# RWKV core: the triangular inverse through four quarters of the array, its X update in bank 6

## What is computed

```python
def step(state, inp):
    r_t, w_t, k_t, v_t, kk_t, b_t = inp
    sk = jnp.einsum('bhvk,bhk->bhv', state, kk_t)
    state = (state * w_t[:, :, None, :] - sk[..., None] * b_t[:, :, None, :]
             + v_t[..., None] * k_t[:, :, None, :])
    return state, jnp.einsum('bhvk,bhk->bhv', state, r_t)
...
_, o = lax.scan(step, s0, (seq_first(r_h), seq_first(w_h), seq_first(k_h), seq_first(v_h),
                           seq_first(kk), seq_first(kk * a_h)))
```

## Time and profile before

| | us |
|---|---|
| median of 3 runs | 3152.23 (3150.76 to 3156.98) |
| span of the profiled execution | 3153.8 |
| PE busy in it | 2975.0 (94%) |
| DVE, POOL, ACT busy | 1542.3, 865.3, 588.5 |
| the RWKV core's blocks, first LT product to the last copy of O | 1038 to 1343 |

### The profile page before, as it was taken

One profiled execution on the slowest core, in us unless ns is written; L12 is line 12 of the kernel. 1 busy time (PEld: TensorE's weight loads), 2 busy tenths in 40 slices (PEclk: granted clock), 3 DMA queues, 4 the chain that ended last, 5 costly groups with the idle time before them and its releaser, 6 DMA issues. The chain is left out here.

```text
span 3153.8 us, 52317 instructions
## 1 busy us (share of the span) xinstructions
PE 2975.0 (94%) x22150; PEld 2086.0 (66%) x22150; DVE 1542.3 (49%) x2520; ACT 588.5 (19%) x1102; POOL 865.3 (27%) x591
## 2 busy tenths in 40 slices
PE   9999999999999899999999998999879998999998
PEld 6845857986887688658566685677768844443433
DVE  5764756336555467534777664764644332111112
ACT  2142040012001333210100002221443211110101
POOL 1111222111121545211899790011245310000000
PEclk9999999999999899999999999999999998999999
DMA  4342223220321000042334452132200017999996
GB/s 165 94 165 77 80 82 113 81 80 28 127 87 47 3 3 4 36 135 74 126 127 148 155 164 80 56 102 68 74 9 3 22 60 271 381 409 409 409 409 272
DMA packets 122230, 412.64 MB, mean 131 GB/s; under 512 B 13568, under 2 KB 21376, under 8 KB 121744
## 3 DMA queue, kind: packets, MB, share of 16 engines
q1 hardware_dynamic: 112784, 373.64, 33.3%
q0 software_dynamic: 9216, 35.66, 3.4%
HBM read 404.97 MB, written 4.28 MB: 130 GB/s over the span
## 5 line engine op out<-in xcount | busy, mean ns | idle before, releaser
L947 PE MATMUL ps<-arena 128*128 128x256 f32 x4760 | 1044.3, 381 | 18.0 <-PEq L905 6.8
L947 PEld LDWEIGHTS ps<-arena 128*128 128x128 f32 x4760 | 898.8, 191 | 173.9 <-issue 43.9
L1003 PE MATMUL ps<-arena 128*128 128x512 f32 (+1 forms) x752 | 291.5, 546 | 10.4 <-DVE arena L1342 7.3
L885 POOL TENSOR_TENSOR arena<-arena 128x512 f32<-128x512 f32 x68 | 94.1, 1384 | 555.9 <-DVE arena L903 190.5
L1003 PEld LDWEIGHTS ps<-arena 128*128 128x128 f32 x752 | 144.3, 193 | 149.6 <-issue 138.7
L3895 PE MATMUL ps<-arena 128*64 128x512 f32 x1024 | 224.8, 594 | 9.7 <-DMA arena<-in_w_up 7.2
L891 POOL TENSOR_TENSOR arena<-arena 128x512 f32<-128x512 f32 x68 | 86.5, 1271 | 484.7 <-PE ps L947 484.7
L1247 DVE TENSOR_TENSOR arena<-ps,arena 128x256 f32<-128x256 f32 x85 | 36.1, 425 | 331.1 <-PE ps L947 330.1
L1178 DVE SCALAR_TENSOR_TENSOR arena<-ps,params,arena 128x511 f32<-128x511 f32 (+4 forms) x266 | 190.7, 717 | 13.5 <-ACT arena L1079 4.4
L4039 POOL TENSOR_SCALAR arena<-arena,small 128x1024 f32<-128x1024 f32 x64 | 191.5, 2992 | 10.1 <-DMA arena<-in_w_mod 6.4
L3895 PEld LDWEIGHTS ps<-arena 128*64 128x64 f32 x1024 | 83.7, 137 | 149.2 <-issue 148.8
(11 more groups left out here) (453 smaller groups left out, 4047.6 us busy)
## 6 DMA issues: line engine op xcount, KB each, us to landing
arena<-in_w_in SPq DMA_DIRECT2D x166, 512.0 KB, 3.7
arena<-in_w_gate SPq DMA_DIRECT2D x128, 512.0 KB, 15.5
arena<-in_w_up SPq DMA_DIRECT2D x128, 512.0 KB, 15.3
arena<-in_w_down SPq DMA_DIRECT2D x128, 512.0 KB, 15.4
arena<-in_w_mod POOLq DMA_DIRECT2D x48, 512.0 KB, 4.2
arena<-in_ffn_up SPq DMA_DIRECT2D x44, 512.0 KB, 4.0
arena<-in_w_branch SPq DMA_DIRECT2D x32, 512.0 KB, 3.6
arena<-spill POOLq DMA_DIRECT2D x16, 640.0 KB, 5.3
```

Source lines behind the costliest of these rows:

```text
L885: vec.tensor_tensor(plane(u, n), part(u, 1, 0), part(u, 1, 1), ALU.add).then_inc(sem, 1)
L947: last = nc.tensor.matmul(k.bank(b)[:, 0:HT], lhs[:, q * P:(q + 1) * P], rhs[:, q, :], start=(first and q == 0), stop=(q == 3), skip_group ...
L1003: last = nc.tensor.matmul(out[0:j["m"], 0:j["n"]], w[:, q * m:(q + 1) * m], j["rhs"](q), start=(n == 0), stop=(n == kn - 1))
```

## The change

- X and XT are kept mirrored to each other. XT keeps the layout of before (partition half = half q of the chunk, columns by head), X and Y take the other (partition half = head h, columns by q). So Y = LM times XT and XT's update X times Y go from each half to both, over four quarters into banks 0 and 1 (level 5: banks 2 and 3). The new helpers are `to_heads` and `to_chunks`. X0 (a product with the identity) and Y5, XT5 go the same way.
- X's own update (X1 to X4) is `in_heads`: two quarters, into bank 6. Bank 6 is also that of the spread norms, the turned O and the bonus, so waits are added in both directions.
- The order on a level is Y, XT, X instead of Y, X, XT.
- `step_lt` makes L twice, as it is and transposed, the second into columns 256 to 511 of the same banks. On DVE it is three operations as before; the mirrored L (`LS`) is what POOL masks for the levels.
- B's order is Y5, trv, XT5, Lk, trkap, trkt, LkV, trbt, NU0, WT, Ak, Ab, with Y5 and XT5 on both banks.
- The turn of O moves from beat 10 to 9, weighed from 12 to 10, the bonus from 14 to 13, its addition from 15 to 14. In the last block they stay at 7, 12, 11 and 15.

```diff
@@ -2025,7 +2025,7 @@
...
-    LT, LM, X, XT, Y = (lambda p, n=n: own(5 * (p % 2) + n) for n in range(5))
+    LS, LM, X, XT, Y = (lambda p, n=n: own(5 * (p % 2) + n) for n in range(5))
@@ -2041,11 +2041,15 @@
...
-    two_banks = lambda b: k.ps[:, b:b + 2, 0:256].rearrange("p h (i c) -> p h i c", i=TT)
+    two_banks = lambda b, o=0: k.ps[:, b:b + 2, o:o + 256].rearrange("p h (i c) -> p h i c", i=TT)
+    pair = lambda ap: ap.rearrange("p (n c) -> p n c", n=2)
+    both = lambda b: k.ps[:, b:b + 2, 0:256]
+    turned_cell = lambda q, i: slice(256 * q + 64 * i, 256 * q + 64 * i + 64)
...
-    strict, incl, ident = k.const("strictC"), k.const("inclC"), k.const("identC")
-    level = lambda n: k.const("levelC")[:, 64 * n:64 * n + 64]
+    strict, incl, ident, after = k.const("strictC"), k.const("inclC"), k.const("identC"), k.const("strictTC")
+    level = lambda n: k.const("levelTC")[:, 64 * n:64 * n + 64]
+    first_level = k.const("levelC")[:, 0:64]
@@ -2061,11 +2065,13 @@
...
-    A = ["X0"] + [f"{s}{n}" for n in (1, 2, 3, 4) for s in ("Y", "X", "XT")]
-    B = ["trv", "Y5", "trkap", "XT5", "Lk", "trkt", "LkV", "trbt", "NU0", "WT", "Ak", "Ab"]
-    B_BEAT = [0, 0, 2, 2, 3, 4, 5, 6, 6, 7, 9, 11]
-    B_BANKS = [(3,), (2,), (3,), (2,), (2, 3), (3,), (2,), (3,), (2,), (2, 3), (2, 3), (2, 3)]
+    A = ["X0"] + [f"{s}{n}" for n in (1, 2, 3, 4) for s in ("Y", "XT", "X")]
+    B = ["Y5", "trv", "XT5", "Lk", "trkap", "trkt", "LkV", "trbt", "NU0", "WT", "Ak", "Ab"]
+    B_BEAT = [0, 1, 2, 3, 4, 5, 5, 6, 6, 7, 9, 11]
+    B_BANKS = [(2, 3), (2,), (2, 3), (2, 3), (2,), (3,), (2,), (3,), (2,), (2, 3), (2, 3), (2, 3)]
+    X_BANK = 6
...
+    TURN_BEAT, WEIGHED_BEAT, BONUS_BEAT, ADDED_BEAT = (9, 7), (10, 12), (13, 11), (14, 15)
@@ -2132,11 +2138,11 @@
...
-            def products(l, r, b):
+            def products(l, r, b, at=0):
...
-                        ins = nc.tensor.matmul(k.bank(b + h)[half(q), 64 * i:64 * i + 64], l[half(h), t], r[half(h), t], start=True, stop=True)
+                        ins = nc.tensor.matmul(k.bank(b + h)[half(q), at + 64 * i:at + 64 * i + 64], l[half(h), t], r[half(h), t], start=True, stop=True)
@@ -2146,12 +2152,26 @@
...
-            def blocks64(l, r, b):
-                for h in range(2):
+            def to_heads(l, r, b):
+                for i in range(TT):
+                    for q, h in ((0, 0), (1, 1), (0, 1), (1, 0)):
+                        other = k.const("ident")[half(q), half(q)] if r is None else r[half(q), cell(h, i)]
+                        ins = nc.tensor.matmul(k.bank(b + q)[half(h), 64 * i:64 * i + 64], l[half(q), cell(h, i)], other, start=True, stop=True)
+                return ins
+
+            def to_chunks(l, r, b):
+                for i in range(TT):
+                    for h, q in ((0, 0), (1, 1), (0, 1), (1, 0)):
+                        t = turned_cell(q, i)
+                        ins = nc.tensor.matmul(k.bank(b + h)[half(q), 64 * i:64 * i + 64], l[half(h), t], r[half(h), t], start=True, stop=True)
+                return ins
+
+            def in_heads(l, r, b):
+                for q in range(2):
...
-                        for q in range(2):
-                            other = k.const("ident")[half(q), half(q)] if r is None else r[half(q), cell(h, i)]
-                            ins = nc.tensor.matmul(k.bank(b)[half(q), cell(h, i)], l[half(q), cell(h, i)], other, start=True, stop=True)
+                        for h in range(2):
+                            t = turned_cell(q, i)
+                            ins = nc.tensor.matmul(k.bank(b)[half(h), t], l[half(h), t], r[half(h), t], start=True, stop=True)
@@ -2164,25 +2184,34 @@
...
-                b = A.index(s) % 2
+                n = int(s[-1])
...
-                    ins = blocks64(XT(p), None, b)
+                    ins = to_heads(XT(p), None, 0)
...
-                    n = int(s[1:])
...
-                    pe.wait_ge(*a_out(p, f"X{n - 1}"))
-                    ins = blocks64(LM(p), X(p), b)
+                    pe.wait_ge(*a_out(p, f"XT{n - 1}" if n > 1 else "X0"))
+                    ins = to_heads(LM(p), XT(p), 0)
...
-                    pe.wait_ge(*a_out(p, "Y" + s[2:]))
-                    ins = blocks64(Y(p), XT(p), b)
+                    pe.wait_ge(*a_out(p, f"Y{n}"))
+                    if n > 1:
+                        pe.wait_ge(*a_out(p, f"X{n - 1}"))
+                    ins = to_chunks(X(p), Y(p), 0)
...
-                    pe.wait_ge(*a_out(p, "Y" + s[1:]))
-                    if s != "X1":
-                        pe.wait_ge(*a_out(p, f"XT{int(s[1]) - 1}"))
-                    ins = blocks64(XT(p), Y(p), b)
+                    pe.wait_ge(*a_out(p, f"Y{n}"))
+                    if n == 1:
+                        pe.wait_ge(kap_ok, min(p + 2, PAIRS))
+                        if p >= 1:
+                            pe.wait_ge(*a_out(p - 1, "X4"))
+                    else:
+                        pe.wait_ge(*a_out(p, f"X{n - 1}"))
+                    if p >= 3 and n == 3:
+                        pe.wait_ge(weighed, p - 2)
+                    if p >= 3 and n == 4:
+                        pe.wait_ge(bonus_ok, p - 2)
+                    ins = in_heads(Y(p), X(p), X_BANK)
@@ -2196,11 +2225,12 @@
...
-                    pe.wait_ge(*a_out(p, "X4"))
-                    ins = cells(LM(p), X(p), b)
+                    pe.wait_ge(*a_out(p, "XT4"))
+                    ins = to_heads(LM(p), XT(p), b)
...
-                    ins = cells(Y(p), XT(p), b)
+                    pe.wait_ge(*a_out(p, "X4"))
+                    ins = to_chunks(X(p), Y(p), b)
@@ -2266,7 +2296,8 @@
...
-                products(pl(a + p), pl(sg + p), 2).then_inc(lt_made, 1)
+                products(pl(a + p), pl(sg + p), 2)
+                products(pl(sg + p), pl(a + p), 2, 256).then_inc(lt_made, 1)
@@ -2340,16 +2371,21 @@
...
+                        if b >= 2:
+                            pe.wait_ge(*a_out(b - 2, "X4"))
...
-                    if b >= 4 and beat == (10 if b < BLOCKS - 1 else 7):
+                    if b >= 4 and beat == TURN_BEAT[b == BLOCKS - 1]:
...
+                        pe.wait_ge(*a_out(min(b - 1, PAIRS - 1), "X2" if b < PAIRS + 1 else "X4"))
...
-                    if b >= 4 and beat == (14 if b < BLOCKS - 1 else 11):
+                    if b >= 4 and beat == BONUS_BEAT[b == BLOCKS - 1]:
...
+                        if b < PAIRS + 1:
+                            pe.wait_ge(*a_out(b - 1, "X3"))
@@ -2384,7 +2420,7 @@
...
-                nc.scalar.activation(Y(p) if s[0] == "Y" else X(p), k.bank(A.index(s) % 2), ACT.Copy).then_inc(a_act, 1)
+                nc.scalar.activation(pair(Y(p) if s[0] == "Y" else X(p)), both(0), ACT.Copy).then_inc(a_act, 1)
@@ -2393,8 +2429,10 @@
...
+                elif s == "Y5":
+                    ins = nc.scalar.activation(pair(Y(p)), both(2), ACT.Copy)
...
-                    dst = {"Y5": Y(p), "trv": VT(p), "trkap": KAPT, "trkt": KT_(p), "trbt": BT_(p), "LkV": LKV}[s]
+                    dst = {"trv": VT(p), "trkap": KAPT, "trkt": KT_(p), "trbt": BT_(p), "LkV": LKV}[s]
@@ -2467,7 +2505,7 @@
...
-                tt(eight(LM(p)), eight(LT(p)), mask8(level(n)), ALU.mult).then_inc(lm_ok if n <= 4 else lm5_ok, 1)
+                tt(eight(LM(p)), eight(LS(p)), mask8(level(n)), ALU.mult).then_inc(lm_ok if n <= 4 else lm5_ok, 1)
@@ -2530,7 +2568,10 @@
...
-                nc.vector.tensor_tensor(x, x, k.bank(A.index(s) % 2), ALU.subtract).then_inc(a_dve, 1)
+                if s[1] == "T":
+                    nc.vector.tensor_tensor(pair(x), pair(x), both(0), ALU.subtract).then_inc(a_dve, 1)
+                else:
+                    nc.vector.tensor_tensor(x, x, k.bank(X_BANK), ALU.subtract).then_inc(a_dve, 1)
@@ -2538,7 +2579,7 @@
...
-                    ins = nc.vector.tensor_tensor(XT(p), XT(p), k.bank(2), ALU.subtract)
+                    ins = nc.vector.tensor_tensor(pair(XT(p)), pair(XT(p)), both(2), ALU.subtract)
@@ -2551,10 +2592,10 @@
...
-                nc.vector.tensor_tensor(quad(LT(p)), two_banks(2), mask(strict), ALU.mult).then_inc(lt_read, 1)
+                nc.vector.tensor_tensor(quad(XT(p)), two_banks(2), mask(first_level), ALU.mult)
+                nc.vector.tensor_tensor(quad(LS(p)), two_banks(2, 256), mask(after), ALU.mult).then_inc(lt_read, 1)
...
-                link(nc.vector.scalar_tensor_tensor(out=eight(XT(p)), in0=eight(LT(p)), scalar=-1.0, in1=mask8(level(0)), op0=ALU.mult, op1=ALU.mult))
-                nc.vector.tensor_tensor(eight(XT(p)), eight(XT(p)), mask8(ident), ALU.add).then_inc(lt_out, 1)
+                nc.vector.tensor_tensor(eight(XT(p)), mask8(ident), eight(XT(p)), ALU.subtract).then_inc(lt_out, 1)
@@ -2611,11 +2652,11 @@
...
-                elif beat == 12:
+                elif beat == WEIGHED_BEAT[p == PAIRS - 1]:
...
-                elif beat == 15:
+                elif beat == ADDED_BEAT[p == PAIRS - 1]:
```

## The result

The changed kernel takes 3173.2 us (median of 4 runs, 3167.5 to 3180.5) against 3154.3 for the kernel before, measured beside it (3150.8 to 3157.0): ratio 1.0056, 95% interval 1.0042 to 1.0071. It is slower by 18 us, where 7 were forecast. 3173.2 lies in the range of 3138 to 3177 and above the forecast's own range (3154 to 3166).

The account below looks back on a forecast made before the run. PE was taken to set the pace in beats 5 to 14, chains through ACT and DVE in beats 15 to 4. Block terms of +4.25 us plus clock losses of 1.7 and 1.4 gave +7.3, so 3159.5 us; range 3138 to 3177.

Parts of the forecast that it names:

- The walk through a full block: One full block, from one state product of beat 15 to the next: 36.07 us against 33.65, 2.4 us longer.
- The two new waits: PE waits for DVE's reads of X2 and X3 in bank 6: 0.85 us before the turn, 0.9 before the bonus.
- Blocks 4 to 7: The four full blocks with all parts: 4 x 2.4 = +9.7 us for the order, with clock losses added separately.
- the sum outside them: Other blocks' order terms: block 3 -2.5, block 2 -0.65, block 8 -0.8, block 9 0, block 0 +1.0, block 1 -2.5 us.
- block 2: Walked like the full block and block 3: -0.65 us, with no clock loss charged to it.
- rival A: PE's saving across eight pairs is paid out in full, 36 us: 3116 us. Chance 0.10.
- Block 8: The block without LT and exponentials: 29.0 us against 29.80, so -0.8.
- Block 1: A bare chain of Y, ACT, XT and DVE with X beside it, 22.03 us before: -2.5 us, between 0 and -5.
- block 3: Has chunk steps but no turn and no bonus, 33.40 us before: -2.5 us, plus 0.35 for the clock.
- D: New-form products stay at 0.93 us, so the 0.45 saving is missing: +20 us, or 3180. Chance 0.05.
- B: Waits on bank 6 are covered, four blocks lose 2.6 instead of 9.7: 3152 us, or 3143 if the clock holds. Chance 0.27.
- C: The clock falls around beat 0: 2.0 us more for each of blocks 4 to 7, block 1 gains nothing: 3170. Chance 0.18.

Follow-up runs that it names:

- e4_fill: The changed kernel with 32 unread identity products into bank 6 ahead of trkap in blocks 2 to 7: 3165.9 us, ratio 1.0038 to the kernel before.
- e1_beats: The changed kernel with the turn of O back at beat 10 and the bonus at 14, weighed 11, addition 15: 3156.8 us, ratio 1.0006 to the kernel before.
- e7_turn_only: The changed kernel with only the turn of O back at beat 10, weighed at 11, bonus still at 13: 3162.4 us, ratio 1.0026 to the kernel before.
- e9_dense: The kernel before with 12 four-quarter, then 12 two-quarter steps added back to back ahead of LT in block 2, unread: 3181.1 us in a single run.

## Why the prediction was right in direction and short in size

*The walk through a full block* held. The pieces of blocks 5 and 6, each read where the clock was whole or within 0.02 of it, add up to 36.5 us against 36.07 forecast. (Block 4 ran at 1.00 and took 35.33, as trkap stands 11.41 behind the copy there.) Counted from the O copy: trv 2.99 (forecast 2.79), XT5's read 8.07 (7.97), trkap 12.48 (12.38), from there to WT 7.33 (7.22), WT to the next copy 16.68 (16.47). The two new waits are 0.88 and 0.77 us (0.85 and about 0.9). LT's read to the state product took 2.4 us (2.52). DVE was the engine that I had working through from XT5 to Lk, and it was.

*Blocks 4 to 7* were to lose 9.7 for the order and 2.8 for the clock: 12.5. They lost 12.6 in one profile and 14.1 in the other. An estimate of the split: the order takes 36.5 - 33.65 = 2.85 in each of blocks 5 to 7 and 1.9 in block 4 (35.33 against 34.64 less the 1.2 of its dip before), so 10.5, and the clock the other 2.2 and 3.6. That 4 x 2.4 came so near is in part luck: block 4 lost less than the walk said, the others more. A dip costs 1.4 to 2.75 us and not 1.7 always, and three of the four blocks had one in the first profile, all four in the second (`e4_fill` shows them as the pause's doing).

*The step that failed is the sum outside them, block 2 above all.* It was "walked likewise" to -0.65; it lost 3.5 and 5.4. Block 2 and its first stretch before, then the block in `e4_fill`:

```profile
1061.44:1087.32 25.88, 23.01 (x722) 20.88 (x722) 13.60 (x21) 8.61 (x16) 14.07 (x13) 1.00 0.01 3
1061.44:1066.00 4.56, 4.34 (x125) 4.06 (x127) 4.41 (x6) 1.18 (x3) 1.75 (x3) 1.00 0.01 4
...
1060.71:1087.61 26.90, 21.58 (x834) 18.81 (x827) 13.60 (x21) 8.48 (x15) 13.74 (x12) 1.00 0.02 5
```

Timeline and granted clock of block 2 after:

```profile
1067.17 0.69 PE L2159 MATMUL ps<-arena 64*64 64x64 f32 x32 [1.42 <-DVE arena L2572]
1068.57 0.66 PE L2181 MATMUL ps<-cst,arena 128*128 128x128 f32 x4 [0.71 <-ACT arena L2433]
...
1089.84 0.33 PE L2145 MATMUL ps<-arena 64*64 64x64 f32 x4 [1.18 <-issue]
...
1093.45 0.34 PE L2145 MATMUL ps<-arena 64*64 64x64 f32 x6 [0.96 <-issue]
...
1064.41:1069.00 4.59, 2.46 (x98) 2.20 (x87) 4.31 (x6) 0.60 (x1) 1.25 (x2) 1.00 0.02 4
1069.00:1074.00 5.00, 5.00 (x105) 3.17 (x106) 0.00 (x0) 3.24 (x6) 1.83 (x2) 0.54 0.01 3
```

The block splits at WT, and two terms of the sum are missing.

- *Ahead of WT, the clock.* From LT's read to WT the kernel before takes 18.42 us, `e4_fill` 17.83 with the clock at 1.00: the 0.6 less that was walked. The two profiles of the changed kernel take 19.69 and 21.97, so 1.9 and 4.1 us are the clock's. I had charged the clock to blocks 3 to 7 only, where the trace of before showed dips, and to none that ran at 1.00. Before, PE was busy 4.34 of the first 4.56 us and the clock stayed whole; after, 2.46 of 4.59, and the next five microseconds run at 0.54. That the thinner start makes it fall isn't shown: `e1_beats`, `e4_fill` and `e7_turn_only` have the same order there, with PE as little busy (2.46 or 2.47 of 4.59), and the clock stays at 1.00 for ten microseconds from LT's read.
- *Behind WT, the pauses of dense steps.* From WT to the next LT's read, all at full clock, it is 9.73 and 9.30 us against 7.45. Of it 2.14 and 1.87 are pauses marked as issue (1.18 and 0.96 above). The trace of before has no such pause in the core; the one of after has 3.9 us of them. The 0.48 us of a step came from WT, one step alone among slower work, and `e9_dense` shows that only the first four steps of a dense stretch have it. By that the 36 us of rival A would have shrunk too; how far, nothing measured here says.

*Block 8* was to gain 0.8 and lost 1.2. Its two pauses marked as issue, 0.83 at 1287.91 and 0.44 at 1296.83, add up to as much, but they don't explain it: with the turn back at beat 10 the block takes 28.84 us (`e7_turn_only`) and 28.86 (`e1_beats`), less than the 29.0 of the walk, though 0.8 and 1.5 us of such pauses stand in it. The turn's place cost the 2.2.

*Block 1* gained 2.6 and 1.5 (forecast 2.5), *block 3* 2.7 and 0.3 (forecast 2.5, less 0.35 for the clock). *Block 10*, which the change doesn't touch, lost 1.6 in one profile to the clock and nothing in the other. *Block 0* lies ahead of LT's first read, and I haven't told it apart.

In one sum, first profile and second: block 1 -2.6 and -1.5, block 2 +3.5 and +5.4, block 3 -2.7 and -0.3, blocks 4 to 7 +12.6 and +14.1, block 8 +1.2 and +1.2, block 10 +1.6 and 0: 13.6 and 18.9.

*The rivals.* A and D fell: steps at 0.59 us of weight loads, time not paid out. B fell as a forecast for the change, as both waits stood bare. But the price that it put on them, 7.1 us, was too low: `e1_beats` got back 16. The 0.85 and 0.9 that B took away are 1.75 of the 2.8 us a block that it measured, and the bonus' own 0.95 ahead of LT makes up the rest. Block 8, which B left out, gave 2.2, and there were fewer dips (clock 0.95, 1.00, 0.95, 0.95). C (the clock falling around beat 0) came in one full block of each profile, at a smaller price: in block 7 of the first the 15 us around beat 0 have 0.89, and trkap stands 13.31 behind the copy, 0.8 later, where C counted 2.0 in every block. In block 6 the same 15 us have 1.00.

```profile
1197.80:1212.80 15.00, 10.06 (x316) 7.83 (x316) 11.52 (x21) 6.82 (x11) 5.42 (x6) 1.00 0.01 3
...
1237.00:1252.00 15.00, 11.57 (x316) 9.35 (x316) 10.65 (x19) 6.93 (x11) 4.93 (x5) 0.89 0.02 4
```

And it came in block 2, in the same place of the order, behind Y5 and trv.

By the Trainium skill, TensorEngine Tiling (Array Packing), section "PSUM Bottleneck", the reads of PSUM may come to bound a tiled kernel. Here the reads kept their 0.6 to 0.7 us, and what bounded were the waits for them and, in dense stretches, the supply of instructions.

## What to carry to other kernels

Before giving an engine cheaper steps, ask what its queue does next: a step that must be read before a shared bank is free turns its saving into waiting as soon as independent work stands behind it in order. Look for a pause that is already there and put a step of the chain behind it into it: here one step moved by a few lines (XT1 in the kernel before, 0.9968) was worth more than the rebuild with its beats mended (0.9996). And take a step's price from a stretch as dense as the one it will run in.

## What was unexpected in the hardware

- PE's products came at 58 to 61 ns each over a dozen steps, whatever the form or the width (192 products in 11.2 us at 64 columns, in 11.7 at 128), with a burst of 64 products at 33 ns (2.09 us) ahead of each pause of 1.4 to 1.6 us.
- 32 unread products (2.08 us) in a pause of 2.5 us made the steps behind it faster: 7.33 us in four blocks of four, where up to 10.08 were needed when the clock had fallen in the pause.
- A dip can begin without any single pause above 1.42 us ahead of it (PE busy 2.46 of 4.59 us), and the same order with as little work can pass without one: it fell in two profiles of five.
